# Moving eight output-projection units of a retention branch between the maps of a block attention

## The reference

```python
h = rmsnorm(x, mix_norm_g[l])
rq, rk, rv, rg, mq, mk, mv, ga, gb = jnp.split(h @ w_in[l], offsets, axis=-1)
ret = retention(rq, rk, to_heads(rv, RET_HEADS))
y_a = (from_heads(ret) * jax.nn.silu(rg)) @ ret_w_branch[l]
att = moba_attention(mq, mk, to_heads(mv, MOBA_HEADS), rel_bias)
y_b = from_heads(att) @ moba_w_branch[l]
merged = jax.nn.sigmoid(ga) * y_a + jax.nn.sigmoid(gb) * y_b
x = x + merged @ w_out[l]
```

## Time and profile before

| | us |
|---|---|
| median of 3 runs | 1884.28 (1876.44 to 1884.68) |
| span of the profiled execution | 1880.4 |
| TensorE busy | 1818.2 (97%) |
| ScalarE, VectorE, GpSimd busy | 868.8, 1264.9, 1000.2 |
| map loop | 919.6 to 975.1 |
| `ret_out` units on TensorE | 975.06 to 999.68 |
| `moba_out` units on TensorE | 999.68 to 1014.65 |

### The profile page before, as it was taken

One profiled execution on the slowest core, in us unless ns is written; L12 is line 12 of the kernel. 1 busy time (PEld: TensorE's weight loads), 2 busy tenths in 40 slices (PEclk: granted clock), 3 DMA queues, 4 the chain that ended last, 5 costly groups with the idle time before them and its releaser, 6 DMA issues.

```text
span 1880.4 us, 32518 instructions
## 1 busy us (share of the span) xinstructions
PE 1818.2 (97%) x11582; PEld 1586.9 (84%) x11582; DVE 1264.9 (67%) x2548; ACT 868.8 (46%) x1405; POOL 1000.2 (53%) x431
## 2 busy tenths in 40 slices
PE   5999899998999999999999999999999999999998
PEld 2847579897979997988878999999999988888887
DVE  6586668879546655115233179899999957777776
ACT  3033545444445454542453555644444444554453
POOL 4043146443775444684547778866666654444443
PEclk8999999999999999999999999999999999999999
DMA  8787137786555554542324545544444455555554
GB/s 325 252 304 253 68 137 243 270 278 219 207 197 179 186 188 156 190 168 90 112 92 155 180 171 185 173 145 150 146 151 144 149 178 192 190 193 196 191 192 166
DMA packets 95329, 346.10 MB, mean 184 GB/s; under 512 B 10544, under 2 KB 12032, under 8 KB 94592
## 3 DMA queue, kind: packets, MB, share of 16 engines
q1 hardware_dynamic: 78048, 283.67, 43.8%
q10 hardware_dynamic: 17184, 61.11, 9.0%
HBM read 343.66 MB, written 1.08 MB: 183 GB/s over the span
## 4 chain that ended last, share of the span: by engine, by line
PE 73%; DVE 14%; issue 5%; POOL 3%; DMA 3%; ACT 2%; ACTq 0%; POOLq 0%; DVEq 0%; SPq 0%
PE ps L525 28%; PE ps L574 26%; POOL ring_lo L470 3%; PE ps L509 2%; PE ps L730 2%; PE ps L644 2%; PE ps L797 2%; DMA ring<-stream 2%; PE ps L744 2%; DVE hot_hi_a L2622 2%; PE ps L954 1%; DVE hot_hi_b L2622 1%; DVE hot_lo_a L2623 1%; DVE hot_lo_b L2623 1%; DVE arena L2633 1%
## 5 line engine op out<-in xcount | busy, mean ns | idle before, releaser
L470 POOL TENSOR_TENSOR ring_lo<-ring,ring_hi 128x1024 fp32r<-128x1024 f32 x371 | 899.0, 2428 | 697.9 <-ACT ring_hi L464 696.2
L464 ACT ACTIVATE ring_hi<-ring 128x1024 fp32r<-128x1024 f32 x502 | 531.5, 1059 | 462.7 <-DMA ring<-stream 458.4
L525 PE MATMUL ps<-h_lo,ring_hi 128*128 128x256 f32 x2096 | 294.2, 283 | 0.0
L525 PEld LDWEIGHTS ps<-h_lo,ring_hi 128*128 128x128 f32 x2096 | 270.3, 192 | 0.0
L574 PE MATMUL ps<-ring_hi,e_pair 128*128 128x512 f32 x1024 | 253.7, 389 | 1.7 <-DVE e_pair L2657 1.7
L2657 DVE TENSOR_TENSOR e_pair<-arena,e_pair 128x256 fp32r<-128x256 f32 x128 | 174.5, 1363 | 99.9 <-ACT e_pair L1730 99.6
L574 PEld LDWEIGHTS ps<-ring_hi,e_pair 128*128 128x128 f32 x1024 | 192.1, 188 | 41.9 <-issue 2.1
L470 DVE TENSOR_TENSOR ring_lo<-ring,ring_hi 128x1024 fp32r<-128x1024 f32 x141 | 176.7, 1254 | 38.3 <-ACT ring_hi L464 38.0
L574 PE MATMUL ps<-ring_hi,arena_r 128*128 128x512 f32 x672 | 174.5, 392 | 0.6 <-ACT ring_hi L464 0.6
L525 PE MATMUL ps<-late_r,ring_hi 128*128 128x256 f32 x1136 | 162.6, 286 | 0.0
L525 PE MATMUL ps<-late_r,ring_lo 128*128 128x256 f32 x1136 | 159.5, 283 | 0.0
(11 more groups left out here) (304 smaller groups left out, 2528.6 us busy)
## 6 DMA issues: line engine op xcount, KB each, us to landing
ring<-stream SPq DMA_DIRECT2D x540, 512.0 KB, 3.3
arena<-aside_w ACTq DMA_DIRECT2D x49, 512.0 KB, 4.6
late<-aside_w ACTq DMA_DIRECT2D x21, 512.0 KB, 4.6
resid<-aside_w ACTq DMA_DIRECT2D x10, 512.0 KB, 5.3
arena<-scale_w ACTq DMA_DIRECT2D x8, 512.0 KB, 16.5
arena<-ln_rows ACTq DMA_DIRECT2D x8, 512.0 KB, 5.3
arena<-gate_cols ACTq DMA_DIRECT2D x2, 1024.0 KB, 4.9
arena<-decay ACTq DMA_DIRECT2D x1, 1536.0 KB, 6.8
```

The costliest lines, as they stand in the source:

```text
L464: act.activation(ring_hi[:, s, :], ring[:, s, :], ACT.Copy).then_inc(hi_ready, 1)
L470: eng.tensor_tensor(ring_lo[:, s, :], ring[:, s, :], ring_hi[:, s, :], ALU.subtract).then_inc(lo_ready[s], 1)
L525: m = pe.matmul(ps[:, bank, 0:T], w[:, kc * P:(kc + 1) * P], x[:, kc, :], start=begin, stop=w is w_lo and kc == KC - 1)
```

## The change

The stream's order: the last eight gate units and the eight retention units form a stage `woven` (`WOVEN`). In TensorE's loop the retention units stand at the end of steps 5, 7, 9, 11, 13, 15, 16 and 17 (`RET_AT_MAP`), in bank 4 + m % 2, after the transposes. The value product waits for the two maps it needs (`turned`) instead of for everything in banks 4 and 5. ScalarE makes the quarters of `ret_hi` in steps 0 to 3, VectorE those of `ret_lo` behind maps 1 to 4. VectorE drains each retention unit ungated into `y_a` (which moves to another part of the arena), before the maximum of the next map. Both sigmoids stay behind the loop; when the first is done VectorE multiplies `y_a` by it in four instructions of 512 columns, and then merges `moba_out` as before. ScalarE's rounded copies of `moba_out`'s units stand around the sigmoids: units 0 and 1 ahead of the first, unit 2 between them, unit 3 behind. GpSimd makes the low parts in the new order.

```diff
+WOVEN = [("gate", 16), ("gate", 17), ("gate", 18), ("ret", 0), ("gate", 19), ("ret", 1), ("gate", 20), ("ret", 2),
+         ("gate", 21), ("ret", 3), ("gate", 22), ("ret", 4), ("gate", 23), ("ret", 5), ("ret", 6), ("ret", 7)]
+WOVEN_UNIT = {what: FIRST_UNIT["woven"] + _k for _k, what in enumerate(WOVEN)}
+RET_AT_MAP = {5: 0, 7: 1, 9: 2, 11: 3, 13: 4, 15: 5, 16: 6, 17: 7}
...
-        y_a = area(2048, KC, T)
+        y_a = area(14336, KC, T)
...
                     if m >= 3 and m % 2 == 1:
-                        pe.wait_ge(emptied[4], fills[4].now())
-                        pe.wait_ge(emptied[5], fills[5].now())
+                        pe.wait_ge(emptied[4], turned[m - 3])
+                        pe.wait_ge(emptied[5], turned[m - 2])
                         values(m // 2 - 1)
...
+                        turned.append(fills[b].n)
+                    late_part(m)
...
+            def late_gate(m):
+                if m % 2 == 0 and m < 16:
+                    h_tile(WOVEN_UNIT["gate", 16 + m // 2], h_hi_2, 4)
+            def ret_unit(m):
+                if m not in RET_AT_MAP:
+                    return
+                n = RET_AT_MAP[m]
+                if n == 0:
+                    pe.wait_ge(ret_hi_ready, 4)
+                    pe.wait_ge(ret_lo_ready, 4)
+                b = 4 + m % 2
+                u = WOVEN_UNIT["ret", n]
+                parts_tile(split_unit(u), ret_hi, ret_lo, lambda kc: kc * P, b, u, True)
+                mark["ret_unit", n] = b, fills[b].n
...
-            pe.wait_ge(ret_hi_ready, 4)
-            pe.wait_ge(ret_lo_ready, 4)
-            for n in range(KC):
-                u = FIRST_UNIT["ret_out"] + n
-                parts_tile(split_unit(u), ret_hi, ret_lo, lambda kc: kc * P, 4 + n % 2, u, True)
...
             def beside(m):
                 if m % 2 == 0 and m < 16:
-                    gate_drain(16 + m // 2, bank=4)
-                if m in (3, 5, 7, 9):
-                    f = (m - 3) // 2
-                    if f == 0:
+                    n = 16 + m // 2
+                    unit_hi(act, WOVEN_UNIT["gate", n] + 2)
+                    drain(4, zz[:, 16 + n, :])
+                if m < 4:
+                    if m == 0:
                         act.wait_ge(mix_ready, 1)
-                    act.activation(ret_hi[:, 2 * f:2 * f + 2, :], ret[:, 2 * f:2 * f + 2, :], ACT.Copy).then_inc(ret_hi_ready, 1)
-                if m in (15, 16):
-                    unit_hi(act, FIRST_UNIT["ret_out"] + m - 15)
+                    act.activation(ret_hi[:, 2 * m:2 * m + 2, :], ret[:, 2 * m:2 * m + 2, :], ACT.Copy).then_inc(ret_hi_ready, 1)
+                if m in RET_AT_MAP:
+                    unit_hi(act, WOVEN_UNIT["ret", RET_AT_MAP[m]] + 2)
+                    drains[4 + m % 2].add()
             attention(16, exp_m, evac_m, beside)
...
+            beside(17)
+            act.activation(zz[:, 24:32, :], zz[:, 24:32, :], ACT.Sigmoid).then_inc(gate_exp, 1)
+            unit_hi(act, FIRST_UNIT["moba_out"] + 2)
+            act.activation(zz[:, 32:40, :], zz[:, 32:40, :], ACT.Sigmoid).then_inc(gate_exp, 1)
+            unit_hi(act, FIRST_UNIT["moba_out"] + 3)
...
-                if m in (5, 7, 9, 11):
-                    f = (m - 5) // 2
+                if 1 <= m <= 4:
+                    f = m - 1
...
+            def ret_drain(n):
+                b, fill = mark["ret_unit", n]
+                dve.wait_ge(full[b], fill)
+                dve.tensor_copy(y_a[:, n, :], ps[:, b, 0:T]).then_inc(emptied[b], 1)
+
+            for m in range(17):
+                behind_ret = m - 1 in RET_AT_MAP
+                if m < 16 and not behind_ret:
+                    max_m(m)
+                if m >= 1:
+                    norm_and_low(m - 1)
+                if behind_ret:
+                    ret_drain(RET_AT_MAP[m - 1])
+                    if m < 16:
+                        max_m(m)
+                if m >= 4 and m % 2 == 0:
+                    values_m(m // 2 - 2)
+            ret_drain(6)
+            values_m(7)
+            ret_drain(7)
...
             dve.wait_ge(gate_exp, 1)
-            for n in range(KC):
-                b, fill = branch_bank("ret_out", n)
-                dve.wait_ge(full[b], fill)
-                dve.tensor_tensor(y_a[:, n, :], ps[:, b, 0:T], zz[:, 24 + n, :], ALU.mult).then_inc(emptied[b], 1)
+            for q in range(4):
+                y = y_a[:, 2 * q:2 * q + 2, :]
+                step(dve.tensor_tensor(y, y, zz[:, 24 + 2 * q:26 + 2 * q, :], ALU.mult))
+            settle()
             dve.wait_ge(gate_exp, 2)
```

More of the change, by code:

```diff
@@ L86 @@
 STAGES = [("ada0", EARLY_ADA), ("proj", N_PROJ), ("attn_out", 8), ("mlp0", 64),
-          ("conv_in", 24), ("conv_out", 8), ("mlp1", 64), ("in2_qk", 16), ("in2_v", 12), ("in2_gates", 24),
-          ("ret_out", 8), ("moba_out", 4), ("out2", 8), ("peer_q", 16), ("peer_keys", 2),
+          ("conv_in", 24), ("conv_out", 8), ("mlp1", 64), ("in2_qk", 16), ("in2_v", 12), ("in2_gates", 16),
+          ("woven", 16), ("moba_out", 4), ("out2", 8), ("peer_q", 16), ("peer_keys", 2),
           ("peer_u", N_EXP), ("peer_v", N_EXP)]
@@ L94 @@
     N_UNITS += _n
+WOVEN = [("gate", 16), ("gate", 17), ("gate", 18), ("ret", 0), ("gate", 19), ("ret", 1), ("gate", 20), ("ret", 2),
+         ("gate", 21), ("ret", 3), ("gate", 22), ("ret", 4), ("gate", 23), ("ret", 5), ("ret", 6), ("ret", 7)]
+WOVEN_UNIT = {what: FIRST_UNIT["woven"] + _k for _k, what in enumerate(WOVEN)}
+RET_AT_MAP = {5: 0, 7: 1, 9: 2, 11: 3, 13: 4, 15: 5, 16: 6, 17: 7}
 PROJ_UNIT = [FIRST_UNIT["proj"] + _n for _n in range(N_PROJ)]
 SPLIT_STAGES = ("attn_out", "mlp0", "conv_in", "conv_out", "mlp1",
-                "in2_qk", "in2_v", "in2_gates", "ret_out", "moba_out", "out2", "peer_q", "peer_u", "peer_v")
+                "in2_qk", "in2_v", "in2_gates", "woven", "moba_out", "out2", "peer_q", "peer_u", "peer_v")
 IS_SPLIT = [_name in SPLIT_STAGES for _name, _n in STAGES for _ in range(_n)]
@@ L807, in _, with attention @@
             n_attn, n_qk = Count(), Count()
-            def attention(n_maps, scores, keys_of, at_t, values, early=None, late_part=None):
+            def attention(n_maps, scores, keys_of, at_t, values, early, late_part):
+                turned = []
                 for m in range(n_maps + 2):
@@ L813, in attention @@
                         scores(m)
-                    if early is not None:
-                        early(m)
+                    early(m)
                     if m >= 3 and m % 2 == 1:
-                        pe.wait_ge(emptied[4], fills[4].now())
-                        pe.wait_ge(emptied[5], fills[5].now())
+                        pe.wait_ge(emptied[4], turned[m - 3])
+                        pe.wait_ge(emptied[5], turned[m - 2])
                         values(m // 2 - 1)
@@ L828, in attention @@
                         fills[b].add()
-                    if late_part is not None:
-                        late_part(m)
+                        turned.append(fills[b].n)
+                    late_part(m)
             pe.wait_ge(h_dve, 1)
@@ L1140, in values_m @@
                     fills[b].add()
-            attention(16, scores_m, lambda k: k % 2 + 1, lambda k, kt: m_attn[:, k % 2, kt * P:(kt + 1) * P],
-                      values_m, lambda m: gate_tile(16 + m // 2, 4) if m % 2 == 0 and m < 16 else None)
-            pe.wait_ge(ret_hi_ready, 4)
-            pe.wait_ge(ret_lo_ready, 4)
-            for n in range(KC):
-                u = FIRST_UNIT["ret_out"] + n
-                parts_tile(split_unit(u), ret_hi, ret_lo, lambda kc: kc * P, 4 + n % 2, u, True)
-            mark["ret_out"] = (fills[4].n, fills[5].n)
+            def late_gate(m):
[12 more added lines that the diff above has]
+                mark["ret_unit", n] = b, fills[b].n
+            attention(16, scores_m, lambda k: k % 2 + 1, lambda k, kt: m_attn[:, k % 2, kt * P:(kt + 1) * P],
+                      values_m, late_gate, ret_unit)
             pe.wait_ge(att_ready, 4)
@@ L1649, in _, with gate_drain @@
             first_hi("in2_gates")
[L1651 to L1655, removed]
+            def gate_drain(n, func=ACT.Copy):
+                unit_hi(act, FIRST_UNIT["in2_gates"] + n + 2)
+                drain(4 + n % 2, zz[:, 16 + n, :], func)
             roots(32)
@@ L1685, in beside @@
                 if m % 2 == 0 and m < 16:
-                    gate_drain(16 + m // 2, bank=4)
-                if m in (3, 5, 7, 9):
-                    f = (m - 3) // 2
-                    if f == 0:
+                    n = 16 + m // 2
[3 more added lines that the diff above has]
+                    if m == 0:
                         act.wait_ge(mix_ready, 1)
-                    act.activation(ret_hi[:, 2 * f:2 * f + 2, :], ret[:, 2 * f:2 * f + 2, :], ACT.Copy).then_inc(ret_hi_ready, 1)
-                if m in (15, 16):
-                    unit_hi(act, FIRST_UNIT["ret_out"] + m - 15)
```

(35 more changed lines are left out.)

## The result

The changed kernel takes 1893.59 us (median of 8 runs, 1891.87 to 1896.69) against 1884.29 (8 runs): a ratio of 1.005, 95% interval 1.0033 to 1.0067, or 6 to 13 us more. Its profiled execution has a span of 1891.9 us, 11.5 over that of before.

The account below looks back on a forecast made before the run. TensorE is busy nearly throughout, VectorE limits the merge. First merge 5.0 us later, plus 1.0 clock in the merge and 0.7 at the first woven unit: 6.7 on 1884.3, so 1891.0 us; range 1880 to 1896.

Parts of the forecast that it names:

- Loop: Block-attention loop: a gate unit every 9.3 us; the relaxed value-product wait saves 1.3 us over five pairs.
- Front: Before the first woven retention unit: TensorE waits 1.9 us because ret_lo subtractions meet GpSimd's work (bounds 0.6 and 1.9).
- End of the loop: From the last gate unit to moba_out: closed gaps save 0.9 us, retention units starting at full clock 1.6.
- First merge: VectorE's first moba_out merge at 1006.4 against 1001.38, 5.0 us later, through late sigmoids and gatings waiting on GpSimd.
- Clock in the merge: In moba_out, after a 7.7 us TensorE gap: one half at 2.9 us instead of 1.44, costing 1.0.
- Clock at the first woven unit: After the 1.9 us wait at retention unit 0: a possible clock fall, price 0 or 1.6 us, taken 0.7.
- 1: Gatings behind the loop: VectorE isn't held up by GpSimd; +0.5 us, 1884.8 us; chance 0.2.
- 2: moba_out's merge: clock stays low, not back within the first two halves; 5.5 us instead of 1.0, 1895.5 us; chance 0.1.
- 3: Behind the loop: sigmoids early enough and all stalls go; first merge 1.7 us behind moba_out's first product, 1881.1 us; chance 0.1.

Follow-up runs that it names:

- e5_wait_alone: Kernel before, only with the value product waiting for its two turned maps; 91.61 us from map 0's gate unit to out2, against 94.34 before.
- e2_low_odd: Changed kernel with the ret_lo quarters made two behind map 1 and two behind map 3; 98.75 us from map 0's gate unit to out2, against 101.07.
- b_again: Kernel before, profiled once more without an edit; 92.86 us from map 0's gate unit to out2, against 94.34 in its first profile.
- e1_pool_holds: Changed kernel with GpSimd making moba_out's third and fourth low parts only after VectorE's four wide gatings; 1890.57 us, ratio 1.003.
- e9_sigmoid_first: Changed kernel with the first sigmoid ahead of ScalarE's copy of moba_out's second unit; 101.10 us from map 0's gate unit to out2, against 101.07.
- e8_gap_short: Changed kernel with 7 idle TensorE products put into the gap between moba_out's first and second unit; median 1891.78 us.
- e3_gate_at_drain: Changed kernel with ga's sigmoid at ScalarE's gate drains and VectorE gating each woven retention unit straight from PSUM; 1890.14 us, ratio 1.0027.
- e7_both_mended: Changed kernel with ret_lo made behind maps 1 and 3, and ga's sigmoid and the gating done at the drains; 1884.95 us, ratio 1.0002.
- e6_wide_in_old_place: Kernel before, retention units still behind the loop but drained raw and gated wide afterwards; 97.94 us from map 0's gate unit to out2, against 94.34.

## Why the prediction was right, step by step

Forecast +6.7 us and 1891.0; measured +9.3 and 1893.59, in the range. The profile gives 6.73 between G and O (+5.09 up to V, +1.64 behind it). That this agrees to 0.03 is luck, in two ways: 0.7 for a clock fall that did not come made up for a clock term in the merge that was 0.6 too small, and the kernel before had a fall in its first profile that it does not have in the second.

- **Loop**: a pair of units 9.36 against 9.3; the relaxed wait 1.24 against 1.3 (e5_wait_alone).
- **Front**: 1.88 against 1.9, with GpSimd as the holder (e2_low_odd).
- **End of the loop**: 0.9 of gaps and 1.6 of clock were to be gained. The gaps close (the one left is 0.61) and are worth 0.6. The 1.6 of clock were read off one profile, and there I failed: of four profiles of before and its descendants only the first has that fall, at 1.5 us (79.37 against b_again's 77.88). Against b_again, G to M is 0.1 longer, not 1.35 shorter, and G to O 8.2 longer, not 6.7. That the timed 9.3 lies above my 6.7 fits this: 8.2, plus four sixths of 1.5 us for the fall at the first woven unit (below), less a quarter of 1.5 for the one at the end of the loop, is 8.8, an estimate from few profiles.
- **First merge**: 8.14 us behind M against 8.6 (1006.4 - 997.8). Third and fourth gating 2.85 and 2.82, as the pattern of the earlier trace rows had them; e1_pool_holds shows the cause. That sigmoids and copy order weigh on it was true of the dates and false as a loss: e9_sigmoid_first takes 3.2 us off the gate's date for nothing. Of the 6.4 us of loss in M to V 4.3 are waits on GpSimd (6.81 - 2.50); the other 2.1 are the gatings' own 2.5, less the 0.4 by which they begin (M + 1.29) ahead of where the first merge stood before (M + 1.70). Without the waits 0.3 of the 4.3 would stay, as the second sigmoid is last then (4.08 in e1_pool_holds). Before, the gating stood in the shadow of TensorE's units.
- **Clock in the merge**: 1.6 against 1.0 (e8_gap_short). I counted one half at the low clock; there were two.
- **Clock at the first woven unit**: taken 0.7 between 0 and 1.6. In the profile of after it cost nothing; of six kernels with that wait the clock fell in four, at 1.5 us.
- **Rivals**: 1 fell with e1_pool_holds; 2 did not come, though the sign that I had given for it, a clock that is not back within two halves, did: the clock was back within the third, and the price was 1.6, not 5.5. 3 did not come, and could not at its price: the four gatings stand behind the last unit's drain, at M + 0.8 at the earliest (e9_sigmoid_first), and take 2.5 us by themselves, so the first merge can't be 1.7 us behind M.

The Trainium skill (GPSIMD Engine Reference, Key points) names contention between GpSimd and VectorE instructions with two SBUF inputs, and this case's trace agrees: 2.85 us instead of 0.68 with two, 0.42 with one operand in PSUM. By that passage one could tell that the new gating may be held and the old one not; how much, and so whether the loss outweighs the gains in the loop, only the rows tell.

**Open**: e3_gate_at_drain and e7_both_mended are timed some 2 to 5 us above what G to O says against before (0.2 and -3.3 against the first profile, 1.7 and -1.8 against b_again; measured, by the ratios, 5.1 and 0.4). The intervals are 1.9 to 8.1 and -2.1 to 3.0, so for e7_both_mended chance can be all of it, for e3_gate_at_drain hardly. The mean granted clock of the timed runs says a little more: 0.9884 over the 12 of e3_gate_at_drain against 0.9907 over the 23 of before beside them, 0.9901 against 0.9901 for e7_both_mended. So e3_gate_at_drain did run with more low clock, 0.0023 of 1884 us or some 4 us at most (an estimate); at which places is not shown, as only one of its runs, one of the fastest, has a profile.

## What to carry to other kernels

Before fusing PSUM drains into wider SBUF instructions, look at what GpSimd does at that time: here an elementwise instruction of VectorE's with two SBUF inputs waited out the GpSimd instruction under way (2.85 us instead of 0.68), one with a PSUM operand did not (0.42). When work is taken from behind a loop, ask what it covered there (here two sigmoids and the gating), and which date opens the next stage. And read a clock fall in one profile as one draw: take a second profile before putting it in a sum.

## What the hardware showed that I had not expected

- VectorE and GpSimd take turns: two gatings 0.6 us apart, then GpSimd's, then one, then GpSimd's; GpSimd pays too: 2.53 us instead of 2.38 to 2.41, and 2.87 in e9_sigmoid_first, where its instruction starts at 1002.81, just behind a gating that starts at 1002.78 and takes its usual 0.68.
- Short gaps and the clock: a wait of 1.9 us was followed by a stretch at 1.2 GHz in four of six kernels, one of 3.07 us in e1_pool_holds and one of 4.94 in e6_wide_in_old_place too; without such a gap the loop kept 2.4 GHz in every profile except at the end of the first.
- A product of 512 columns with plain 32-bit operands takes 0.86 us (30 in 25.91, shown as two instructions each), in the form that the units use, from rounded copies, 0.23 (12 of `out2` in 2.72 us, in before).
